# Attention values in the order of the head halves, and expert steps that turn the gathered rows two slots ahead

## The chip, the core and the metric

The kernel runs on one core of a Trainium2 chip. The metric is the time on the device, in microseconds (us), of one execution. Engines are named as the profile names them: PE (TensorE, with PEld for its weight loads), DVE (VectorE), ACT (ScalarE), POOL (GpSimd) and SP (SyncE, which only issues transfers here). Each engine works through its own list of instructions in order and waits on semaphores where it needs another's result.

## The reference

The input has 512 tokens of width 1024. Two blocks follow each other. Cut to what this change touches:

```python
# first block: sliding-window attention (4 heads, 2 key/value heads, blocks of 128 queries) and
# attention over 256 memory rows (4 heads)
out = einsum('bnhgqj,bnjhd->bnqhgd', probs, vb)          # sliding window
out = einsum('bhsm,bmhd->bshd', probs, mem_v)            # memory

# second block: attention over selected keys, 16 heads in 4 groups, 128 queries at a time
p = softmax(where(valid, logits, -inf))
o = einsum('bqhgk,bqkhd->bqhgd', p, v_sel)

# second block, last part: 32 experts (4 groups of 8), two of one group for each token, fp32
for g in range(4):
    a = einsum('nd,edf->nef', hf, w_gate[g])
    u = einsum('nd,edf->nef', hf, w_up[g])
    act = silu(a) * u * combine[:, g, :, None]
    out = out + einsum('nef,efd->nd', act, w_down[g])
return x + out
```

## The kernel before

It is one program for the whole of both blocks, with the list of each engine written out by hand. Nothing schedules it: the order of work on an engine is the order of the code. Two stages are touched.

**Attention.** `attention(...)` is PE's list for both attentions: 8 batches in the first (the four window blocks, then four blocks over the memory), 16 in the second (query block 3 first, then 2, 1 and 0, each for four groups of four heads). A batch b passes through these steps: scores (L764 or L839) into PSUM; DVE takes the maximum (L1656, L1663 or L1820); ACT takes the exponentials (L1173); PE turns the probabilities with a product by the identity (L740), heads 0 and 1 first and then, after the scores of a later batch, heads 2 and 3, through the same PSUM space `p_t`; the turned halves are copied to `pT`, the first by DVE (L1645, semaphore `pT_ready_first`), the second by ACT (L1233, `pT_ready_second`); a small product (L748) spreads the reciprocal of the denominators; the value products (`values1`, L771, or `values2`, L847) go to `p_v`; DVE multiplies them by the reciprocals (L1640, `y_made`). Before its value products PE waits for both halves of `pT` and for `y_made` of the batch before, which frees `p_v`. Keys reach 128 x (query block + 1), so in the second attention a batch has between 1 and 4 blocks of keys, and `values2` has two matmuls for each block, of 256 moving columns: heads 0 and 2 in one, heads 1 and 3 in the other. All of this is fp32; the trace has two records for each fp32 matmul.

**Experts.** The 32 experts are 16 pairs, and 8 further pairs take what exceeds 64 rows of an expert. They make 24 steps; slots 2, 5, 8, ... are the overflow pairs. In step s PE has `project(s)` (L1028: gate and up product of both experts of the pair, 16 matmuls of 512 columns from `xT`), `turn_slot(s + 1)` (L1020: eight transposes of the next slot's gathered rows `xg` into `p_rows`), `down(s - 1)` (L1040: eight matmuls of 512 columns from `actT`) and two transposes of the activations of step s (L1061). DVE copies `p_rows` to the single `xT` (L2148, after `turned` and after `gu_done` of the step, since `project` reads `xT`), and multiplies the activations (L2196). ACT applies silu (L1509), copies the down product to `yg` (L1503) and the turned activations to `actT` (L1513). POOL issues the indirect transfers: the gather of slot s + 3 (L1103, three buffers `xg`, after `turned`), at each third step, once the down product of the slot two back is done, the six transfers for the next overflow pair's weights (L1110, L1113), and the scatter of each slot's result (L1120). SP issues the plain loads of 1 MiB each for the weights: two of gate and up per expert after `gu_done` (L480), one of down per expert after `dn_done` (L483); `w_gu` and `w_dn` have three pairs of buffers. The step of index 0 has in addition a product that sorts the overflow rows (L1055).

Of the kernel before, what the change touches and what calls it, by code (L numbers as in the profile page):

```python
# [13 lines left out]
P = 128  # L14
# [8 lines left out]
HD = 64  # L23
# [14 lines left out]
STEPS = PAIRS + OVER_PAIRS  # L38
# [103 lines left out]
def program(nc, d, out):  # L142
# [11 lines left out]
    with ExitStack() as ctx:  # L154
# [30 lines left out]
        p_s, p_t, p_v, p_r = ps[1], ps[0][:, 0:2, :], ps[0][:, 2, :], ps[0][:, 3, :]  # L185


        base = -(-nc.sbuf_base // 64) * 64
# [40 lines left out]
        kvt = at("kvt", 48, [P, TT, 512])  # L229
# [284 lines left out]
        def _(pe):  # L514
# [119 lines left out]
            s = turns.take()  # L634
# [65 lines left out]
            def attention(batches, scores, values, nkb, pr, pT, base, first=None, beside=None):  # L700
# [8 lines left out]
                for i in range(batches + 2):  # L709
# [10 lines left out]
                            next(chunks)  # L720
                    b = i - 2
                    if 0 <= b < batches:
                        for half in range(2):
                            pe.wait_ge(pT_ready[half], base + b + 1)
                        if base + b > 0:
                            pe.wait_ge(y_made, base + b)
                        values(b, p_v).then_inc(v_full, 1)
                    b = i - 1
                    if 0 <= b < batches:
                        for half in range(2):  # L730
# [33 lines left out]
                    last = pe.matmul(s[:, h, 0:k.shape[1]], q, k, start=True, stop=True)  # L764
                return last

            def values1(b, out):
                blocks = 1 if b == 0 else 2
                for h, kb in ((2 * c + odd, kb) for c in range(2) for kb in range(blocks) for odd in range(2)):
                    v = sv1[:, max(b - 1, 0) + kb, HD * (h // 2):HD * (h // 2 + 1)] if b < 4 else mv[:, kb, HD * h:HD * (h + 1)]  # L770
                    last = pe.matmul(out[HD * (h % 2):HD * (h % 2 + 1), P * (h // 2):P * (h // 2 + 1)], v,  # L771
                                     pT1[:, h, P * kb:P * (kb + 1)], start=(kb == 0), stop=(kb == blocks - 1))
                return last
# [66 lines left out]
                                     kT2[g // 2][lanes, g % 2, 0:P * (n + 1)], start=True, stop=True)  # L840
                return last

            def values2(b, out):
                n, g = query_block(b), b % 4
                for kb in range(n + 1):
                    for odd in range(2):
                        last = pe.matmul(out[HD * odd:HD * (odd + 1), 0:256].rearrange("p (c t) -> p c t", c=2),  # L847
                                         kvt[:, kb, 256 + HD * g:256 + HD * (g + 1)], pT2[:, odd:4:2, P * kb:P * (kb + 1)],
                                         start=(kb == 0), stop=(kb == n))
                return last  # L850

# [109 lines left out]
            s = job()  # L961
# [53 lines left out]

            def turn_slot(s):

                pe.wait_ge(xg_in[s % 3], 16 * (s // 3 + 1))
                for k in range(KC):
                    last = pe.transpose(p_rows[:, k // 4, P * (k % 4):P * (k % 4 + 1)], xg[s % 3][:, k:D:KC], ident[:])  # L1020
                last.then_inc(turned, 1)
# [23 lines left out]
            for s in range(STEPS):  # L1045
                pe.wait_ge(xT_ready, s + 1)
                if s > 0:
                    pe.wait_ge(act_ready, s)
                project(s)
                if s + 1 < STEPS:  # L1050
                    turn_slot(s + 1)
                if s == 0:
                    pe.wait_ge(rt_step, 4)
                    for i in range(2 * TT):
                        last = pe.matmul(p_over, hot_r[:, i, :], over_c[:, i, :], start=(i == 0), stop=(i == 2 * TT - 1))  # L1055
                    last.then_inc(over_made, 1)
                if s > 0:
                    down(s - 1)
                pe.wait_ge(act_ready, s + 1)
                for f in range(2):  # L1060
                    last = pe.transpose(p_act[:, P * f:P * (f + 1)], act[:, f:HID:2], ident[:])  # L1061
                last.then_inc(act_turned, 1)
# [1160 lines left out]
```

## Time and profile before

| | |
|---|---|
| median of 3 runs | 1455.56 us (1453.52 to 1459.57) |
| the profiled execution | 1457.66 us, its span in the profile 1455.8 us |
| granted TensorE clock, mean of the span | 0.969 of full speed |
| PE busy | 1328.3 us, 91% of the span |
| POOL, DVE, ACT busy | 678.5, 579.4, 363.5 us |
| value products of the second attention (L847) | 160 records |
| gate and up products (L1028), busy | 172.0 us, 768 records |
| down products (L1040), busy | 87.6 us, 384 records |

A row of a timeline has the start, the duration, the engine, the line, the operation, output<-input, the tile's shape and how many instructions were merged; in brackets stands how long the engine had been idle and what released it. The durations of matmuls are modelled at their end, so that a matmul's record overlaps the next one's start by some 0.1 us: where a step's length matters it is read from one start to the next. In a line of waits the numbers are the total, the number of times and the longest. A release named "issue" is one for which the profile shows no other engine.

The first attention lies between about 183 and 227 us, the second between about 485 and 595 us, the experts between about 1128 and 1432 us.

### The profile page before, as it was taken

To read this page: it belongs to the slowest core of one execution; us is meant where nothing else is said; L and a number is where in the kernel's file an instruction comes from. 1 tells how busy PE (TensorE), PEld (TensorE's weight loads), DVE (VectorE), ACT (ScalarE), POOL (GpSimd) and SP (SyncE) were. 2 spreads that over 40 slices of the span, in tenths; PEclk is the share of its full clock that TensorE was granted. 3 is DMA by queue.
4 is the path that set the end of the run, shared out by engine and by line. 5 is a ranking of instruction groups with operands and counts; after the bars stand their busy time and mean duration, and the time that the engine had idled before them with its cause. 6 is when DMAs were issued, how large, how long until landed. Compare 5 with 4: busy or idle time off the path is not lost.

```text
span 1455.8 us, 18220 instructions
## 1 busy us (share of the span) xinstructions
PE 1328.3 (91%) x7169; PEld 954.5 (66%) x7169; DVE 579.4 (40%) x930; ACT 363.5 (25%) x707; POOL 678.5 (47%) x711
## 2 busy tenths in 40 slices
PE   5999979899899999999998888999995999999993
PEld 5887857777677666788887877888874333333330
DVE  1232262527891265534855566542314311111112
ACT  3201062402322277112123433231013011111110
POOL 6557513755547400676773233765851333333320
PEclk9999989999999999999999999999997999999997
DMA  5523210422123300134322113532273598999954
GB/s 207 147 73 116 66 51 7 139 98 88 60 85 116 112 6 1 58 95 145 108 72 73 44 44 131 222 140 87 87 317 131 192 384 354 366 372 369 373 220 188
DMA packets 85449, 216.34 MB, mean 149 GB/s; under 512 B 23716, under 2 KB 32628, under 8 KB 71796
## 3 DMA queue, kind: packets, MB, share of 16 engines
q1 hardware_dynamic: 62124, 199.22, 37.1%
q0 software_dynamic: 13824, 8.44, 2.0%
q10 hardware_dynamic: 9416, 7.51, 1.6%
q8 instruction: 57, 0.93, 0.3%
q14 instruction: 28, 0.23, 0.0%
HBM read 255.99 MB, written 26.22 MB: 194 GB/s over the span
## 4 chain that ended last, share of the span: by engine, by line
PE 78%; DVE 4%; ACT 4%; DMA 4%; issue 3%; POOL 2%; ACTq 2%; DVEq 1%; POOLq 0%; SPq 0%
PE ps L137 17%; PE ps L139 16%; PE ps L138 16%; PE ps L1028 9%; PE ps L1040 5%; DMA w_gu<-w_up,over_u 2%; PE ps L922 2%; PE ps L740 2%; PE ps L1020 2%; PE ps L847 1%; POOL w_lo L1073 1%; PE ps L839 1%; ACTq L1440 1%; DMA xg<-rows_scratch,row_u 1%; PE ps L748 1%
## 5 line engine op out<-in xcount | busy, mean ns | idle before, releaser
L1070 POOL CAST w_hi<-stage 128x512 fp32r<-128x512 f32 (+1 forms) x296 | 188.4, 678 | 490.3 <-PE ps L139 477.7
L1073 POOL TENSOR_TENSOR w_lo<-stage,w_hi 128x512 fp32r<-128x512 f32 (+1 forms) x296 | 386.5, 1337 | 10.8 <-issue 0.4
L137 PE MATMUL ps<-hi,w_hi 128*128 128x512 f32 (+1 forms) x600 | 234.8, 391 | 9.9 <-ACTq L1323 2.5
L139 PE MATMUL ps<-lo,w_hi 128*128 128x512 f32 (+1 forms) x600 | 233.3, 389 | 0.0
L138 PE MATMUL ps<-hi,w_lo 128*128 128x512 f32 (+1 forms) x600 | 233.1, 388 | 0.0
L137 PE MATMUL ps<-w_hi,hi 128*128 128x512 f32 (+2 forms) x520 | 187.9, 361 | 13.0 <-ACTq L1440 7.6
L138 PE MATMUL ps<-w_hi,lo 128*128 128x512 f32 (+2 forms) x520 | 186.3, 358 | 0.0
L139 PE MATMUL ps<-w_lo,hi 128*128 128x512 f32 (+2 forms) x520 | 186.2, 358 | 0.0
L1028 PE MATMUL ps<-w_gu,xT 128*64 128x512 f32 x768 | 172.0, 600 | 5.7 <-DMA w_gu<-w_up,over_u 4.3
L137 PEld LDWEIGHTS ps<-hi,w_hi 128*128 128x128 f32 x600 | 113.5, 189 | 37.6 <-issue 6.6
L139 PEld LDWEIGHTS ps<-lo,w_hi 128*128 128x128 f32 x600 | 113.3, 189 | 23.1
L138 PEld LDWEIGHTS ps<-hi,w_lo 128*128 128x128 f32 x600 | 113.6, 189 | 22.6
L2148 DVE TENSOR_TENSOR xT<-ps,ffn_kp 128x1024 f32<-128x1024 f32 x24 | 29.4, 1224 | 245.3 <-PE ps L1020 245.3
L1028 PEld LDWEIGHTS ps<-w_gu,xT 128*64 128x64 f32 x768 | 55.2, 138 | 104.8 <-issue 100.8
L137 PEld LDWEIGHTS ps<-w_hi,hi 128*128 128x128 f32 x520 | 100.7, 194 | 30.0 <-ACTq L1440 8.3
L139 PEld LDWEIGHTS ps<-w_lo,hi 128*128 128x128 f32 x520 | 100.6, 193 | 13.9
L138 PEld LDWEIGHTS ps<-w_hi,lo 128*128 128x128 f32 x520 | 100.6, 193 | 13.7 <-issue 0.2
L1040 PE MATMUL ps<-w_dn,actT 128*64 128x512 f32 x384 | 87.6, 598 | 1.0 <-ACT actT L1513 1.0
L1120 POOL DMA_INDIRECT y_scratch<-yg,out_u x24 | 24.2, 1007 | 114.2 <-ACT yg L1503 112.0
L1040 PEld LDWEIGHTS ps<-w_dn,actT 128*64 128x64 f32 x384 | 25.5, 136 | 45.5 <-issue 41.7
L1509 ACT ACTIVATE sa<-ps 128x256 f32<-128x256 f32 x24 | 9.2, 383 | 170.1 <-PE ps L1028 170.1
L1820 DVE CUSTOM_DVE_ANT_0 pr<-ps,sel 128x512 f32<-128x512 f32 (+3 forms) x64 | 27.6, 487 | 59.4 <-PE ps L839 53.8
(437 smaller groups left out, 1691.5 us busy)
## 6 DMA issues: line engine op xcount, KB each, us to landing
stage<-w_in SPq DMA_DIRECT2D x84, 512.0 KB, 4.5
w_gu<-w_gate SPq DMA_DIRECT2D x32, 1024.0 KB, 12.2
w_gu<-w_up SPq DMA_DIRECT2D x32, 1024.0 KB, 14.5
w_dn<-w_down SPq DMA_DIRECT2D x32, 1024.0 KB, 11.2
stage<-w_out SPq DMA_DIRECT2D x16, 512.0 KB, 4.5
stage<-w_ssd_branch SPq DMA_DIRECT2D x16, 512.0 KB, 4.5
stage<-w_in SPq DMA_DIRECT2D x20, 256.0 KB, 3.1
stage<-w_attn_branch SPq DMA_DIRECT2D x8, 512.0 KB, 4.3
```

What stands on the lines that cost most here:

```text
L137: pe.matmul(out, x[0], w[0], start=first, stop=False)
L138: pe.matmul(out, x[1], w[0], start=False, stop=False)
L139: return pe.matmul(out, x[0], w[1], start=False, stop=last)
L740: last = pe.transpose(p_t[:, h % 2, P * kb:P * (kb + 1)], pr(b)[:, h, P * kb:P * (kb + 1)], ident[:])
L922: last = pe.matmul(ps[s][:, h // 8, HD * (h % 8):HD * (h % 8 + 1)], decay[:, h, :], xd[:, h, :], start=True, stop=True)
L1020: last = pe.transpose(p_rows[:, k // 4, P * (k % 4):P * (k % 4 + 1)], xg[s % 3][:, k:D:KC], ident[:])
L1028: last = pe.matmul(p_gu[h], xT[:, k, h], w_gu[b][:, :, k, :], start=(k == 0), stop=(k == KC - 1))
L1040: last = pe.matmul(p_dn[h, c, :], actT[:, f, h], w_dn[b][:, f, 512 * c:512 * (c + 1)], start=(f == 0), stop=(f == 1))
L1070: nc.gpsimd.tensor_copy(hi[:, b, k, 0:n], stage[:, b, k, 0:n])
L1073: last = nc.gpsimd.tensor_tensor(lo[:, b, k, 0:n], stage[:, b, k, 0:n], hi[:, b, k, 0:n].bitcast(F32), ALU.subtract)
L1820: V.tensor_tensor_reduce(pr2[:, i % 2, h, 0:width], p_s[:, h, 0:width], sel[:, n, 0:width], 1.0, -3e38, ALU.add, ALU.max, sm[:, 0, k, h:h ...
L2148: V.tensor_tensor(xT[:], ps[0][:, 2:4, :].rearrange("p c (k t) -> p (c k) t", t=P), bc(ffn_kp[:], 2, P), ALU.mult)\
```

## The change

Two independent edits.

In `attention`, PE waits for `y_made` first, then for `pT_ready_first`, then runs the value products of heads 0 and 1 (half 0), then waits for `pT_ready_second`, then runs those of heads 2 and 3. `values2` therefore has matmuls of 128 moving columns, one per head and block of keys, twice as many as before; `values1` has the same matmuls as before, called half by half.

In the expert steps, step 0 and 1 still turn slot s + 1 behind `project(s)`. From step 1 on the rows of slot s + 2 are turned behind `down(s - 1)`, directly ahead of the transposes of the activations, and `turn_slot` waits until DVE has emptied `p_rows` (`xT_ready`). In steps 2 to 21 nothing stands between `project(s)` and `down(s - 1)`.

```diff
                     b = i - 2
                     if 0 <= b < batches:
+                        if base + b > 0:
+                            pe.wait_ge(y_made, base + b)
                         for half in range(2):
                             pe.wait_ge(pT_ready[half], base + b + 1)
-                        if base + b > 0:
-                            pe.wait_ge(y_made, base + b)
-                        values(b, p_v).then_inc(v_full, 1)
+                            last = values(b, half, p_v)
+                        last.then_inc(v_full, 1)
...
-            def values1(b, out):
+            def values1(b, c, out):
                 blocks = 1 if b == 0 else 2
-                for h, kb in ((2 * c + odd, kb) for c in range(2) for kb in range(blocks) for odd in range(2)):
+                for h, kb in ((2 * c + odd, kb) for kb in range(blocks) for odd in range(2)):
...
-            def values2(b, out):
+            def values2(b, c, out):
                 n, g = query_block(b), b % 4
                 for kb in range(n + 1):
                     for odd in range(2):
-                        last = pe.matmul(out[HD * odd:HD * (odd + 1), 0:256].rearrange("p (c t) -> p c t", c=2),
-                                         kvt[:, kb, 256 + HD * g:256 + HD * (g + 1)], pT2[:, odd:4:2, P * kb:P * (kb + 1)],
+                        last = pe.matmul(out[HD * odd:HD * (odd + 1), P * c:P * (c + 1)],
+                                         kvt[:, kb, 256 + HD * g:256 + HD * (g + 1)], pT2[:, 2 * c + odd, P * kb:P * (kb + 1)],
                                          start=(kb == 0), stop=(kb == n))
                 return last
...
             def turn_slot(s):
+                if s > 0:
+                    pe.wait_ge(xT_ready, s)
                 pe.wait_ge(xg_in[s % 3], 16 * (s // 3 + 1))
...
                 project(s)
-                if s + 1 < STEPS:
+                if s < 2:
                     turn_slot(s + 1)
...
                 if s > 0:
                     down(s - 1)
+                    if s + 2 < STEPS:
+                        turn_slot(s + 2)
                 pe.wait_ge(act_ready, s + 1)
```

PE's list in the second attention, one batch of query block 3 before (from the second half of a batch's transposes to the scores of another; `pr` are the probabilities, `sm` the reciprocals, `kvt` the values):

```order
L740 MATMUL ps<-ident,pr_107 128x128 [waits pT_ready_first]
L740 MATMUL ps<-ident,pr_107 128x128 x7
L748 MATMUL ps<-ident,sm 64x128 [waits share_ready,den_ready]
L748 MATMUL ps<-ident,sm 64x128 x3
L847 MATMUL ps<-pT_106,kvt 64x256 [waits y_made,pT_ready_second,pT_ready_first]
L847 MATMUL ps<-pT_106,kvt 64x256 x7
L740 MATMUL ps<-ident,pr_107 128x128 [waits pT_ready_second,exp_ready]
L740 MATMUL ps<-ident,pr_107 128x128 x7
```

And the same place with the change:

```order
L741 MATMUL ps<-ident,pr_107 128x128 [waits pT_ready_first]
L741 MATMUL ps<-ident,pr_107 128x128 x7
L749 MATMUL ps<-ident,sm 64x128 [waits share_ready,den_ready]
L749 MATMUL ps<-ident,sm 64x128 x3
L848 MATMUL ps<-pT_106,kvt 64x128 [waits pT_ready_first,y_made]
L848 MATMUL ps<-pT_106,kvt 64x128 x7
L848 MATMUL ps<-pT_106,kvt 64x128 [waits pT_ready_second]
L848 MATMUL ps<-pT_106,kvt 64x128 x7
L741 MATMUL ps<-ident,pr_107 128x128 [waits pT_ready_second,exp_ready]
L741 MATMUL ps<-ident,pr_107 128x128 x7
```

Eight matmuls of 256 columns became sixteen of 128, and the wait for the second half moved behind the first eight of them.

PE's list in the experts, the end of step 2 before (from the last matmul of its projection to the transposes of its activations):

```order
L1028 MATMUL ps<-w_gu_177,xT 64x512
L1020 MATMUL ps<-ident,xg_184 128x128 [waits xg_in0]
L1020 MATMUL ps<-ident,xg_184 128x128 x7
L1040 MATMUL ps<-w_dn_180,actT 64x512 [waits dn_in3,y_ready,dn_in2,actT_ready]
L1040 MATMUL ps<-w_dn_181,actT 64x512
L1040 MATMUL ps<-w_dn_180,actT 64x512
L1040 MATMUL ps<-w_dn_181,actT 64x512
L1040 MATMUL ps<-w_dn_180,actT 64x512
L1040 MATMUL ps<-w_dn_181,actT 64x512
L1040 MATMUL ps<-w_dn_180,actT 64x512
L1040 MATMUL ps<-w_dn_181,actT 64x512
L1061 MATMUL ps<-ident,act 128x128 [waits act_ready]
```

With the change:

```order
L1031 MATMUL ps<-w_gu_177,xT 64x512
L1043 MATMUL ps<-w_dn_180,actT 64x512 [waits dn_in3,y_ready,dn_in2,actT_ready]
L1043 MATMUL ps<-w_dn_181,actT 64x512
L1043 MATMUL ps<-w_dn_180,actT 64x512
L1043 MATMUL ps<-w_dn_181,actT 64x512
L1043 MATMUL ps<-w_dn_180,actT 64x512
L1043 MATMUL ps<-w_dn_181,actT 64x512
L1043 MATMUL ps<-w_dn_180,actT 64x512
L1043 MATMUL ps<-w_dn_181,actT 64x512
L1023 MATMUL ps<-ident,xg_185 128x128 [waits xg_in1,xT_ready]
L1023 MATMUL ps<-ident,xg_185 128x128 x7
L1066 MATMUL ps<-ident,act 128x128 [waits act_ready]
```

The eight transposes moved behind the down product, and they turn the next slot but one. The lists of the other engines are as before.

## Rows read from the trace of the kernel before

**Rows 1.** Page, part 4: the chain that ended last.

```profile
PE 78%; DVE 4%; ACT 4%; DMA 4%; issue 3%; POOL 2%; ACTq 2%; DVEq 1%; POOLq 0%; SPq 0%
```

**Rows 2.** Timeline, second attention, one batch of query block 3.

```profile
524.08 1.23 DVE L1645 COPY pT<-ps 128x1024 f32<-128x1024 f32 x1 [1.65 <-PE ps L740]
...
525.80 0.42 DVE L1640 TENSOR_TENSOR y<-ps,share 128x256 f32<-128x256 f32 x1 [0.17 <-issue]
...
526.49 0.66 PE L748 MATMUL ps<-ident,sm 128*64 128x128 f32 x8
526.60 1.02 ACT L1233 ACTIVATE pT<-ps 128x1024 f32<-128x1024 f32 x1 [1.34 <-PE ps L740]
...
527.72 1.95 PE L847 MATMUL ps<-pT,kvt 128*64 128x256 f32 x16 [0.57 <-issue]
```

**Rows 3.** Timeline of PE, first attention: matmuls of 128 columns.

```profile
208.35 1.09 PE L771 MATMUL ps<-pT,sv 128*64 128x128 f32 x16
```

**Rows 4.** Waits between 500 and 597 us, those of PE before L847.

```profile
PE ps L847 <- issue: 5.1, 10, 1.2
...
PE ps L847 <- ACT pT L1233: 0.7, 1, 0.7
```

**Rows 5.** Timeline of PE, first attention, values of batch 0.

```profile
193.61 1.12 PE L771 MATMUL ps<-pT,sv 128*64 128x128 f32 x8 [0.91 <-ACT pT L1233]
```

**Rows 6.** Chain in the first attention: start, duration, what.

```profile
213.77 1.50 ACTq L1247
```

**Rows 7.** Timeline of PE, expert step 3.

```profile
1168.90 7.09 PE L1028 MATMUL ps<-w_gu,xT 128*64 128x512 f32 x32
1175.92 1.16 PE L1020 MATMUL ps<-ident,xg 128*128 128x128 f32 x8
1177.01 3.65 PE L1040 MATMUL ps<-w_dn,actT 128*64 128x512 f32 x16
1180.59 0.51 PE L1061 MATMUL ps<-ident,act 128*128 128x128 f32 x2
1181.03 7.09 PE L1028 MATMUL ps<-w_gu,xT 128*64 128x512 f32 x32
```

**Rows 8.** Timeline of PE: step 0, whose transposes meet others, and step 23.

```profile
1139.89 1.16 PE L1020 MATMUL ps<-ident,xg 128*128 128x128 f32 x8
1140.80 1.03 PE L1055 MATMUL ps<-over_c,hot_r 128*128 128x8 f32 x8
...
1416.06 7.09 PE L1028 MATMUL ps<-w_gu,xT 128*64 128x512 f32 x32
1422.97 3.60 PE L1040 MATMUL ps<-w_dn,actT 128*64 128x512 f32 x16
1426.51 0.50 PE L1061 MATMUL ps<-ident,act 128*128 128x128 f32 x2
```

**Rows 9.** Timeline of POOL and PE around slot 3's gather in step 1.

```profile
1153.53 0.99 POOL L1103 DMA_INDIRECT xg<-rows_scratch,row_u  x1 [0.30 <-issue]
...
1156.34 0.50 PE L1061 MATMUL ps<-ident,act 128*128 128x128 f32 x2
```

**Rows 10.** DMA issues, window 1153.3 to 1154.3 us, that gather: count, us to landing.

```profile
xg<-rows_scratch,row_u POOLq DMA_INDIRECT x1, 4.2
```

**Rows 11.** Waits between 1130 and 1440 us: PE for an overflow pair's weights.

```profile
PE ps L1028 <- DMA w_gu<-w_up,over_u: 4.3, 4, 1.3
```

**Rows 12.** Timeline of POOL, and PE's: the second overflow pair's transfers and the projection that needs them.

```profile
1186.72 0.99 POOL L1110 DMA_INDIRECT w_gu<-w_up,over_u  x1 [0.30 <-issue]
...
1194.57 7.09 PE L1028 MATMUL ps<-w_gu,xT 128*64 128x512 f32 x32 [1.35 <-DMA w_gu<-w_up,over_u]
```

**Rows 13.** Windows, steps 1 to 21: us, busy of each engine, PEclk, DMA share, GB/s.

```profile
1143.20:1403.90 260.70, 254.97 (x1219) 97.32 (x1218) 32.98 (x45) 34.69 (x63) 84.05 (x84) 1.00 0.93 364
```

**Rows 14.** Gathers: POOL's issue after the overflow transfers, and the landing of all 24.

```profile
1190.63 1.02 POOL L1103 DMA_INDIRECT xg<-rows_scratch,row_u  x1 [0.30 <-issue]
...
DMA to landing us min/median/max: 3.4/10.0/11.4
```

## The prediction, made before the run

> **What bounds the kernel now.** I read the chain first: PE is 78% of it and no other engine has more than 4% [rows 1]. So time is won only where PE's own list gets shorter or where PE stands still. Next the timelines of the two stages, PE's rows first, then the row of whichever engine released a gap.
>
> In the second attention the reader should see PE finish its small product (start 526.49, modelled 0.66 us), stand still for 0.57 us, and begin the value products at 527.72, 0.10 us after ACT's copy of the second half (526.60 + 1.02 = 527.62). The first half was copied long before (DVE, 524.08 + 1.23 = 525.31), and `y_made` came at 526.22 [rows 2]. The waits name 5.1 us in 10 such gaps and 0.7 us in one more [rows 4].
>
> In the experts PE is nearly gapless. Step 3 is 7.02 (projection) + 1.09 (turn) + 3.58 (down) + 0.44 (activations) = 12.13 us from start to start [rows 7]. A matmul row's modelled end overlaps the next start by 0.07 (7.09 against 7.02). The only other losses are four waits for an overflow pair's weights, 4.3 us [rows 11], while the DMA engines are busy for 0.93 of the stage [rows 13].
>
> **Value products, second attention.** 160 records become 320, the columns stay. The price of a 128-column record comes from two rows of the same shape: 16 take 1.09, 8 take 0.66 [rows 2, 3], so one more costs (1.09 - 0.66)/8 = 0.054. Sixteen of 256 columns take 1.95 [rows 2]; thirty-two of 128 would take 1.09 + 16 x 0.054 = 1.95. The finer cut is free as long as the second half follows without a pause. I take 0; if each second half began afresh it would pay 1.09 - 16 x 0.054 - 0.07 = 0.16, for 16 batches 2.6 us.
>
> The gaps to be filled are 5.8 us, and each is 0.07 longer than its row says, because idle is counted from the modelled end: 11 x 0.07 = 0.8, so 6.6 us [rows 4]. Two can't be filled whole: the longest (1.2 + 0.07), since half a batch covers about 1.0 of it, leaves 0.3; the one behind ACT (0.7 + 0.07), where half a batch of one key block covers 0.3, leaves 0.5. That is 5.8. In the middle batches ACT's and DVE's own work nearly fills the shorter period; I take off 0.3 as an estimate: **5.5 us**, between 6.6 - 0.8 - 2.6 - 0.3 = 2.9 and 7.0. `y_made`, now waited for first, comes 0.85 before PE could start (526.22 against 526.49 + 0.66 - 0.07), so it holds nothing.
>
> *A rule against it.* The row says 0.054 us for a further 128-column product with its weight load. The Trainium skill ("TensorE: Matmul & The Clock Gate", section "Back-to-back issue gap") states sustained spacings of about 81 ns at 128 columns and 131 ns at 512. By an estimate from that page 320 products would take 25.9 us and 160 of 256 columns about 98 ns each, 15.7 us; the edit would pay 10.2 us to fill the gaps. The trace disagrees at 128 columns, and the sum goes by the trace.
>
> **Value products, first attention.** Counts don't change. Batch 0 waits 0.91 us for ACT before its 8 records [rows 5]; one half (about 0.5) moves into that gap: 0.5. In batches 4 to 7 the chain runs through ACT releasing the scores' PSUM (1.50 us as one piece [rows 6]), and an earlier value product is worth nothing there; only the last three batches have PE on the chain, about 0.2 each. **1.1 us**, between 0 and 1.4.
>
> **Expert steps.** No instruction is added or removed; three borders change.
> - Projection directly ahead of down: in step 23 the projection takes 1422.97 - 1416.06 = 6.91 instead of 7.02, and the down product behind it 1426.51 - 1422.97 = 3.54 instead of 3.58 [rows 7, 8]. 0.15.
> - Turn directly ahead of other full-width products: in step 0 the eight transposes take 1140.80 - 1139.89 = 0.91 instead of 1.09 [rows 7, 8]. 0.18.
>
> So 0.33 for each of steps 2 to 21, 6.6 us; step 1 has only the second (0.18), step 22 only the first (0.15): 6.9 us. The vacated place also frees `xT` and the activations earlier: DVE's copy starts as the projection ends and lies beside the 3.54 us of down.
>
> What the move costs: slot 3 is now turned at the end of step 1. Its gather is issued at 1153.53 and lands 4.2 us later, at 1157.73; PE arrives at 1156.34 [rows 9, 10]. PE waits 1.4 to 1.5 us, and the activations of step 1 and the whole of step 2 queue behind it. **Minus 1.5**; if it landed in the shortest time seen, 3.4 [rows 14], 0.6; if like the longest, 11.4, 8.6. Nothing else is in flight then, so I stay near 4.2. For later slots: the gather behind the overflow transfers is issued 1190.63 - 1180.59 = 10.0 us after its down product, and its rows are needed two steps later, 2 x 11.8 = 23.6; even 11.4 us to land leaves 2.2.
>
> The overflow weights: their transfers start when a down product ends, and the projection that needs them comes 0.44 + 12.13 = 12.57 later now, afterwards (0.91 + 0.44) + 6.91 + 3.54 + (0.91 + 0.44) = 13.15, so 0.58 more room. If they land by their own issue, the four waits shrink by 2.3. But the plain loads are released by the end of the projection ahead, and from there to the same point the way gets shorter, 17.24 to 16.69. The last needed transfer is issued at 1186.72 and PE starts at 1194.57, 7.8 later, though a gather alone lands in 4.2 [rows 10, 12]: it stands behind plain loads. Three steps contain 0.93 x 36.4 = 33.9 us of transfers [rows 13] and will last 3 x 11.8 = 35.4. If the backlog rules, six waits grow by 0.55 each: 3.3. I take **minus 1.0**, nearer the backlog.
>
> The Trainium skill ("DMA: Bandwidth & Descriptors", section "Queues, rings and completion order") says that each DMA engine takes turns between its queues packet by packet. By that POOL's transfers would not have to let the plain loads finish, the waits would shrink by those 2.3, and the total would be 3.3 better. The 7.8 against 4.2 speaks only half for it.
>
> Experts: 6.9 - 1.5 - 1.0 = **4.4 us**, between 6.9 - 1.5 - 3.3 = 2.1 and 6.9 - 0.6 + 2.3 = 8.6.
>
> **Sum.** 5.5 + 1.1 + 4.4 = 11.0 us. The profiled execution took 1457.66 (span 1455.8), 2.1 over the median shown; I subtract from the median: 1455.56 - 11.0 = **1444.5 us**. The bounds together give 1438.5 to 1450.6; the stages between are PE's and should pass a gain on.
>
> **Rivals.**
> 1. *The experts turn into a DMA stage.* For: share 0.93, and each load is released by PE, so that the queues run empty for a while in every three steps whatever PE does. Against: 33.9 us fit into 35.4. Then the shorter steps come back as longer waits on `w_gu`, and the stage gives nothing: 1448.9.
> 2. *The second attention is not PE's.* ACT or DVE would take the place of the gap. For: their rows fill most of a batch. Against: ACT stood idle 1.34 and DVE 1.65 in the batch shown [rows 2]. Half a gain, 2.0 instead of 5.5: 1448.0.
> 3. *The finer products are slow.* If a 128-column product cost what the rows of the transposes give, 0.91/8 = 0.114 each [rows 8], 320 would take 36.5 instead of 320 x 0.054 = 17.3: 19.2 paid and 5.8 filled, so 13.4 lost instead of 5.5 won: 1463.4, slower. It decides above (17.3 + 5.8 + 5.5)/320 = 0.089 us each. Against: the records of [rows 3] have the very shape. By the Trainium skill's spacings, above, 10.2 would be paid and 5.8 filled, 4.4 lost, and the time 1454.4; with the trace against it that has 0.02.
> 4. *Gathers late behind the loads*, in each third step; it needs more than 13.5 us to land, and 11.4 is the longest. With 16 us six stalls of 2.5 us: 1459.5.
> 5. *More than I count*: the waits on overflow weights vanish and the borders in the attention also shorten: 1439.
>
> **Chances.** Forecast with its own bounds (1440 to 1449) 0.60; the first rival 0.15, the second 0.08, the third 0.03 (and 0.02 for its case by the Trainium skill), the fourth 0.03, the fifth 0.09. To hold the time 8 times in 10 the range reaches from 1438.5 to 1451.5. Within 0.5% is within 7.3 us, about what a measurement of this kernel tells from no change: faster than 1448.3 has 0.57 + 0.05 + 0.05 + 0.09 = 0.76, slower than 1462.8 the third and a part of the fourth, 0.04, the rest 0.20.
>
> **What would show it.** In the second attention PE's rows should run from the small product straight into the first half, with no "issue" ahead of it, batches of block 3 some 0.6 us shorter, and 320 records with some 0.055 between starts. In the experts a step of 11.8 us, transposes and activations 1.35 together, one wait on the gather in step 1 of 1.5 us, and waits on `w_gu` of 3 to 8 us in all. I am wrong if the steps stay at 12.1, if the waits on `w_gu` or `xg` exceed 10 us, or if ACT's idle in the attention goes to nothing while the batches keep their length.

## The result, and the profile after

| | before | changed |
|---|---|---|
| median | 1455.07 us (1453.52 to 1459.57, 4 runs) | 1439.71 us (1438.15 to 1444.75, 4 runs) |
| profiled execution (span) | 1457.66 us (1455.8 us) | 1438.15 us (1436.3 us) |
| granted TensorE clock, mean | 0.969 | 0.971 |

The ratio is 0.9893 [0.9865, 0.9922]: the change takes 15.6 us off, between 11.3 and 19.6 by the interval. The forecast was 1444.5 us (11.0 off), its range 1438.5 to 1451.5.

The chain of the changed kernel, page, part 4, which answers to [rows 1]:

```profile
PE 77%; ACT 5%; DMA 5%; DVE 5%; issue 3%; POOL 2%; ACTq 2%; DVEq 1%; POOLq 0%; SPq 0%
```

PE still bounds the kernel, so again only PE's rows have to be followed. To compare two executions I cut PE's list into stretches by landmarks that both have (first score product of each attention, product behind the last values, first projections, last down product) and took the differences of start times:

| stretch, us | before | changed | difference |
|---|---|---|---|
| start to the first attention | 182.75 | 181.90 | -0.85 |
| first attention | 44.38 | 43.06 | -1.32 |
| from there to the second | 257.72 | 255.25 | -2.47 |
| second attention | 110.14 | 103.82 | -6.32 |
| to the projection of step 0 | 535.99 | 535.80 | -0.19 |
| projection 0 to projection 1 | 12.22 | 12.28 | +0.06 |
| projection 1 to the last down | 284.77 | 276.75 | -8.02 |

The three touched stages give 1.3 + 6.3 + 8.0 = 15.6 us. The profiled spans differ by 19.5; the other 3.9 lie in stretches that no line of the change touches. That the three stages give the very 15.6 of the medians is chance: further profiles, below, make it 14.0.

*Second attention.* PE's timeline of the changed kernel, the batch that answers to [rows 2] (block 3, the last of its four batches, as there; start, us, engine, line, what):

```profile
519.55 0.66 PE L749 MATMUL ps<-ident,sm 128*64 128x128 f32 x8
...
520.04 1.92 PE L848 MATMUL ps<-pT,kvt 128*64 128x128 f32 x32
...
521.88 0.88 PE L741 MATMUL ps<-ident,pr 128*128 128x128 f32 x6
```

From the small product to the row behind the values it takes 521.88 - 519.55 = 2.33 us. In the kernel before it took 3.11, from 526.49 to the row behind those of [rows 2]:

```profile
529.60 0.66 PE L740 MATMUL ps<-ident,pr 128*128 128x128 f32 x4
```

There is no gap ahead of L848. From the values of the batch in front to these it is 6.02 us (514.02 to 520.04) where it was 6.65 (521.07 to 527.72), so 0.63 of the 0.78 us stay and 0.15 are given back elsewhere in the batch; the prediction had asked for some 0.6. ACT's copy of the second half, which runs 519.66 to 520.68, lies beside the first half of the values:

```profile
519.66 1.02 ACT L1238 ACTIVATE pT<-ps 128x1024 f32<-128x1024 f32 x1 [0.71 <-PE ps L741]
```

PE's group of the values in this attention, by line (busy, mean ns of one, idle time before them and its releasers), in the kernel before:

```profile
L847 PE MATMUL ps<-pT,kvt 128*64 128x256 f32 x160 | 20.8, 387 | 6.1 <-issue 5.1 <-ACT pT L1233 0.7
```

The same in the changed kernel, and there PE's waits before the values (us, times, longest), which answer to [rows 4]:

```profile
L848 PE MATMUL ps<-pT,kvt 128*64 128x128 f32 x320 | 21.9, 276 | 1.0 <-ACT pT L1238 0.8
```

```profile
PE ps L848 <- ACT pT L1238: 0.8, 3, 0.3
```

The idle time before the values fell from 6.1 us to 1.0, and none of it is "issue" any more.

*First attention.* The values of batch 0, which answer to [rows 5], and the chain at a middle batch, which answers to [rows 6]:

```profile
191.64 0.64 PE L772 MATMUL ps<-pT,sv 128*64 128x128 f32 x4
192.68 0.70 PE L772 MATMUL ps<-pT,sv 128*64 128x128 f32 x4 [0.39 <-ACT pT L1238]
193.30 1.12 PE L741 MATMUL ps<-ident,pr 128*128 128x128 f32 x4
```

```profile
207.97 1.50 ACTq L1252
```

Half of batch 0's values went into the gap, and 0.39 of the 0.91 us is left. The middle batches have still the 1.50 us of ACT on the chain, and their period is 4.71 us in both kernels (205.90 to 210.61 before, 204.81 to 209.52 now, PE's score products).

*Experts.* PE's timeline of one step, which answers to [rows 7]:

```profile
1237.48 3.60 PE L1043 MATMUL ps<-w_dn,actT 128*64 128x512 f32 x16
1241.01 1.16 PE L1023 MATMUL ps<-ident,xg 128*128 128x128 f32 x8
1242.00 0.40 PE L1066 MATMUL ps<-ident,act 128*128 128x128 f32 x2
1242.34 7.09 PE L1031 MATMUL ps<-w_gu,xT 128*64 128x512 f32 x32
1249.25 3.60 PE L1043 MATMUL ps<-w_dn,actT 128*64 128x512 f32 x16
```

From start to start: projection 6.91, down 3.53, slot's transposes 0.99, activations' transposes 0.34, together 11.77 (before 7.02 + 3.58 + 1.09 + 0.44 = 12.13). The waits of PE from 1130 us on, which answer to [rows 11]:

```profile
PE ps L1031 <- DMA w_gu<-w_up,over_u: 2.5, 5, 0.6
PE ps L1023 <- DMA xg<-rows_scratch,row_u: 2.3, 1, 2.3
```

Two of the prediction's signs missed here. It asked for 3 to 8 us of waits on `w_gu`, and the row has 2.5; and it placed one wait of 1.5 us on slot 3's rows, while the row is that of slot 2. What the DMA engines did in the steps between projection 1 and projection 22, which answers to [rows 13]:

```profile
1132.10:1386.10 254.00, 249.10 (x1229) 100.73 (x1228) 32.98 (x45) 37.58 (x63) 84.53 (x85) 1.00 0.95 374
```

The share rose from 0.93 to 0.95, as the same transfers in shorter steps must make it.

And step 1, in which slots 2 and 3 are both turned (it answers to [rows 9]):

```profile
1141.46 1.12 PE L1023 MATMUL ps<-ident,xg 128*128 128x128 f32 x8 [2.27 <-DMA xg<-rows_scratch,row_u]
1142.51 3.65 PE L1043 MATMUL ps<-w_dn,actT 128*64 128x512 f32 x16
1146.25 1.13 PE L1023 MATMUL ps<-ident,xg 128*128 128x128 f32 x8
```

The start of slot 3's transposes is 3.74 us behind that of the down product, which takes 3.58 elsewhere: 0.16 us of wait on slot 3 are left.

### The profile page after: what moved, and what is told of

Same layout as the page of the kernel before. It is cut to its first block, busy times and chain, and to the rows that moved or that the text cites. A ratio compares the mean times of both kernels' runs of the same rounds, so it can differ in the third digit from the quotient of the medians.

```text
span 1436.3 us, 18562 instructions
## 1 busy us (share of the span) xinstructions
PE 1318.1 (92%) x7329; PEld 961.5 (67%) x7329; DVE 575.2 (40%) x930; ACT 365.1 (25%) x707; POOL 677.5 (47%) x711
## 4 chain that ended last, share of the span: by engine, by line
PE 77%; ACT 5%; DMA 5%; DVE 5%; issue 3%; POOL 2%; ACTq 2%; DVEq 1%; POOLq 0%; SPq 0%
PE ps L137 17%; PE ps L139 16%; PE ps L138 16%; PE ps L1031 9%; PE ps L1043 5%; DMA w_gu<-w_up,over_u 3%; PE ps L923 2%; PE ps L741 2%; POOL w_lo L1078 1%; PE ps L1023 1%; PE ps L848 1%; PE ps L840 1%; ACT pr L1178 1%; DMA xg<-rows_scratch,row_u 1%; ACTq L1445 1%
## 5 line engine op out<-in xcount | busy, mean ns | idle before, releaser
L1043 PEld LDWEIGHTS ps<-w_dn,actT 128*64 128x64 f32 x384 | 28.8, 137 | 53.6 <-issue 52.3
## 6 DMA issues: line engine op xcount, KB each, us to landing
w_gu<-w_up SPq DMA_DIRECT2D x32, 1024.0 KB, 14.5
```

The costliest lines, as they stand in the source:

```text
L1043: last = pe.matmul(p_dn[h, c, :], actT[:, f, h], w_dn[b][:, f, 512 * c:512 * (c + 1)], start=(f == 0), stop=(f == 1))
```

## The experiments

Seven kernels. All ratios are to the kernel before. The profile of each gives the same stretches as above; where runs of one kernel spread over several us, it is the stretch that tells more than the median.

**The attention's edits alone** (e_attention): the changed kernel with the expert steps of before.

```
-                if s > 0:
-                    pe.wait_ge(xT_ready, s)
...
-                if s < 2:
+                if s + 1 < STEPS:
...
-                    if s + 2 < STEPS:
-                        turn_slot(s + 2)
```

> The kernel before with the attention edit alone. Lengths by starts: second attention (first score product to the product behind the last values) 110.1 us before and 103.8 with both edits; first attention 44.3 and 43.0; the stretch between them 257.8 and 255.3; step 1 to the last down product of the experts 284.8 and 276.7. Theory: the two edits don't touch each other, and the stretch between the attentions varies from run to run by itself. Then the second attention is 103.8 +- 0.3, the first 43.0, the experts stay at 284.8 +- 1, and the time is 7.5 us below before (5 to 10). Rival: a part of the gain is handed on, since after a shorter first attention the stretch behind it also gets shorter (the weights are split further ahead); then that stretch is 255.3 again here, and 257.8 in the kernel with the expert edit alone.

Measured: 1444.6 us (1442.66 to 1449.32, 6 runs), ratio 0.9932 [0.9914, 0.9951], so 9.9 us. The attention stages are 43.26 and 103.84 us long, those of the changed kernel within 0.2; the stretch from projection 1 to the last down is 283.68. The two attentions give 1.1 + 6.3 = 7.4 us by their lengths, which the interval of the ratio (7.1 to 12.5 us) holds as well as the 9.9. The stretch between the attentions is 255.6 here, and 257.9 in the next kernel, which is what the rival had said of a gain handed on; e_fine and e_best speak against it further down. Its PE waits from 1130 us on, with the expert steps of before:

```profile
PE ps L1029 <- DMA w_gu<-w_up,over_u: 2.4, 3, 1.1
PE ps L1021 <- DMA xg<-rows_scratch,row_u: 2.1, 1, 2.1
```

**The expert steps alone** (e_experts): the value products as before.

```
-                            last = values(b, half, p_v)
-                        last.then_inc(v_full, 1)
+                        values(b, p_v).then_inc(v_full, 1)
```

> The kernel before with the expert edit alone. Theory: all that the experts gained is theirs: steps of 11.78 us instead of 12.13, six waits for an overflow pair's weights of 3.0 us in all (2.5 to 3.5) instead of 4.6, 276.7 us from step 1 to the last down product, and a time 8 us below before (6 to 10); the attentions stay at 44.3 and 110.1. Rival: the smaller waits on overflow weights were chance of one execution, since the plain loads in the way are the same; then the waits come out between 4 and 8 us and the stage at 278 to 282.

Measured: 1449.42 us (1447.19 to 1450.7), ratio 0.9963 [0.9948, 0.9977], so 5.4 us, less than expected. Stretches: attention 44.67 and 110.16 (44.38 and 110.14 before), experts 278.02, 6.75 shorter than before. Neither expected answer fits whole: the waits of 3.3 us are still those of the theory, the stage is at the lower edge of the rival's 278 to 282. The two parts add up, 9.9 + 5.4 = 15.3 against 15.6, but each is known to 2 or 3 us only. Its PE waits from 1130 us on:

```profile
PE ps L1030 <- DMA w_gu<-w_up,over_u: 3.3, 3, 1.4
PE ps L1022 <- DMA xg<-rows_scratch,row_u: 2.9, 2, 2.1
```

**The finer products without the overlap** (e_fine): expert steps of before, value products by halves, but both halves awaited ahead of the first.

```
+                        for half in range(2):
+                            pe.wait_ge(pT_ready[half], base + b + 1)
                         for half in range(2):
-                            pe.wait_ge(pT_ready[half], base + b + 1)
                             last = values(b, half, p_v)
```

> Only the finer cut of the value products, with both waits still ahead of the first of them: 320 records of 128 columns in the second attention. Theory: a further product of 128 columns costs 0.054 us, so a batch of four key blocks spends 32 x 0.054 + 0.15 = 1.88 us from its first value product to the next work, as with 16 of 256 columns; second attention 110.1 +- 1 us, time as before. Rival (a weight load paired with each product sets the pace, 0.081 us): 2.6 us for such a batch, 320 x 0.081 = 25.9 against 18, second attention 118 us, time 8 us above before.

Measured: 1455.12 us (1448.77 to 1456.16, 10 runs), ratio 1.0006 [0.9989, 1.0023]; second attention 110.34 us against 110.14, first 44.57 against 44.38. The profiled execution is the fastest of the ten. A batch of block 3 and PE's group in this kernel:

```profile
520.84 0.66 PE L750 MATMUL ps<-ident,sm 128*64 128x128 f32 x8
522.07 1.97 PE L849 MATMUL ps<-pT,kvt 128*64 128x128 f32 x32 [0.57 <-issue]
523.97 0.87 PE L742 MATMUL ps<-ident,pr 128*128 128x128 f32 x6
```

```profile
L849 PE MATMUL ps<-pT,kvt 128*64 128x128 f32 x320 | 21.0, 276 | 6.1 <-issue 5.1 <-ACT pT L1235 0.7
```

The 320 records carry the very idle time that 160 carried before (6.1: 5.1 and 0.7 named, as in [rows 4]), and 32 records take 523.97 - 522.07 = 1.90 us where 16 of 256 columns took 529.60 - 527.72 = 1.88. So the cut into halves is free within 0.2 us a stage, and the attention's gain comes from the overlap it allows. The third rival (slow finer products) is out. The stretch between the attentions is 255.0 us here, without any gain in the first attention. The old expert steps take 282.65 us from projection 1 to the last down, and their PE waits from 1130 us on are a third sample:

```profile
PE ps L1030 <- DMA w_gu<-w_up,over_u: 2.1, 3, 1.2
PE ps L1022 <- DMA xg<-rows_scratch,row_u: 1.5, 1, 1.5
```

**Turning only one slot ahead, behind down** (e_one_ahead): value products as before.

```
-                if s < 2:
+                if s == 0:
...
-                    if s + 2 < STEPS:
-                        turn_slot(s + 2)
+                    if s + 1 < STEPS:
+                        turn_slot(s + 1)
```

> The kernel before with the rows of the next slot, not of the next but one, turned behind the down product from step 1 on; the three borders between kinds of products are then as in the changed kernel, but DVE can fill xT only at the step's end. Theory: the borders win 0.35 us a step, and PE waits in each step for DVE (1.22 for xT, 0.41 for the activations, and 0.2 of hand-overs, less nothing that hides it): 12.13 - 0.35 + 1.8 = 13.6 us a step, experts 284.8 + 22 x 1.45 = 317 us, less 4 for waits on weights that vanish, time 28 us above before. Rival: most of the copy hides behind the transposes of the activations, and a step is 12.3 or less, time within 4 us of before; turning two ahead would then be worth little beyond the borders.

Measured: 1493.94 us (1493.28 to 1494.48), ratio 1.0267 [1.0248, 1.0287], so 39 us slower where 28 were expected; a step takes 13.76 us instead of the expected 13.6, steps 1 and 2 take 16.94 and 16.44. Its waits of PE between 1160 and 1480 us, one step, and DVE's rows in it:

```profile
PE ps L1065 <- DVE act L2200: 36.4, 21, 2.1
```

```profile
1196.02 3.60 PE L1042 MATMUL ps<-w_dn,actT 128*64 128x512 f32 x16
1199.55 1.16 PE L1022 MATMUL ps<-ident,xg 128*128 128x128 f32 x8
1202.42 0.51 PE L1065 MATMUL ps<-ident,act 128*128 128x128 f32 x2 [1.72 <-DVE act L2200]
1202.86 7.09 PE L1030 MATMUL ps<-w_gu,xT 128*64 128x512 f32 x32
```

```profile
1200.82 1.23 DVE L2152 TENSOR_TENSOR xT<-ps,ffn_kp 128x1024 f32<-128x1024 f32 x1 [12.21 <-PE ps L1022]
1201.96 0.41 DVE L2200 TENSOR_TENSOR act<-sa,ps 128x256 f32<-128x256 f32 x1
```

The same order of PE's products with the turn for the next slot instead of the next but one: now DVE's copy of `xT` can begin only when the turn ends, DVE's product for the activations stands behind that copy on its list, and PE waits 1.72 us for it ahead of the activations' transposes in most steps. The wait also takes away the borders between the two kinds of transposes: the eight take 2.87 - 1.72 = 1.15 us (1199.55 to 1202.42), the two 0.44, as when they stood apart. The new place is worth its 0.35 us only because the slot is turned a step earlier.

**Overflow weights issued early** (e_gu_early), and **in another order** (e_gu_first). In both, the overflow pair's transfers are split in `overflow_gu` (four) and `overflow_dn` (two). e_gu_first calls one behind the other in the old place; e_gu_early moves the first ahead of the wait for down:

```
                         pool.wait_ge(gu_done, s)
+                        overflow_gu(s // 3)
                         pool.wait_ge(dn_done, s)
-                        overflow(s // 3)
+                        overflow_dn(s // 3)
```

> The changed kernel, with one thing moved on POOL's list: in each third step the overflow pair's four w_gu transfers are issued as soon as the projection that last read their buffers has ended, and only its two w_dn transfers wait for the down product. The w_gu issues come 3.5 us earlier (the down product's length in the changed kernel). Theory (the remaining waits of PE on overflow weights, 2.5 us in five places of 0.34 to 0.65, are a matter of when POOL issues them): all of them vanish, the stretch from the projection of step 1 to the last down product falls from 276.8 to some 274, and the kernel takes 2.5 to 3 us less than the changed one, a ratio to the kernel before of 0.987. Rival (the plain loads of SP's queue ahead of them set the landing, since the DMA engines are busy 0.93 of the stage or more): the waits stay at 2 to 3 us or move to the w_gu of plain slots, and the ratio is that of the changed kernel, 0.989.

> The changed kernel, with the overflow pair's six transfers in another order and none issued earlier: four w_gu, then two w_dn. The last w_gu goes out as the fourth instead of the fifth, 1.3 us earlier. Theory (landing follows POOL's own issue): a wait of 0.34 to 0.65 us that is 1.3 us late in its issue vanishes, so 2.5 us of waits go to nothing, as with the early issue. Rival (the backlog of plain loads sets the landing): the waits stay between 0.3 and 0.7 us each. Either way the stage moves by 0 to 2.5 us, so the rows of the waits tell, not the time.

Measured: e_gu_early 1437.29 us (1435.9 to 1440.02, 6 runs), ratio 0.9892 [0.9873, 0.9912]; e_gu_first 1437.97 us (1437.31 to 1438.44, 4 runs), 0.9894 [0.987, 0.9918]. By the time neither can be told from the changed kernel. By PE's waits from 1130 us on they can; first e_gu_first, then e_gu_early, which has no row for `w_gu` (nor has e_best, the next kernel):

```profile
PE ps L1031 <- DMA w_gu<-w_up,over_u: 3.0, 4, 1.1
PE ps L1023 <- DMA xg<-rows_scratch,row_u: 2.8, 2, 1.5
```

```profile
PE ps L1023 <- DMA xg<-rows_scratch,row_u: 2.7, 2, 1.5
```

The early issue takes all of the waits away. It is 8.0 us earlier and not the 3.5 that I expected (POOL's first issue of the same pair at 1233.95 us, against 1241.95): the projection that frees the buffers is that of the step before, so POOL doesn't stand at that wait at all, and the four `w_gu` transfers go out ahead of the plain loads, which follow at 1237.83; the two of `w_dn` stay behind, at 1242.03. This edit moves the time and the place ahead of the plain loads together, and no run parts the two. The stretch to the last down falls to 274.16 us (276.75 in the changed kernel, 277.49 in e_gu_first), 2.6 us for the 2.5 of waits. The order alone takes nothing away, though the last `w_gu` leaves 1.3 us earlier. One pair of the changed kernel shows why: POOL's rows, then the landing of the issues at 1245.83 and 1247.13 us and of the last at 1248.42, and PE's row.

```profile
1241.95 0.99 POOL L1115 DMA_INDIRECT w_gu<-w_gate,over_u  x1 [8.47 <-PE ps L1043]
...
1247.13 0.99 POOL L1115 DMA_INDIRECT w_gu<-w_up,over_u  x1 [0.30 <-issue]
1248.42 0.99 POOL L1118 DMA_INDIRECT w_dn<-w_down,over_u  x1 [0.30 <-issue]
```

```profile
w_gu<-w_gate,over_u POOLq DMA_INDIRECT x1, 7.0
...
w_gu<-w_up,over_u POOLq DMA_INDIRECT x1, 7.6
...
w_dn<-w_down,over_u POOLq DMA_INDIRECT x1, 6.4
```

```profile
1254.83 7.09 PE L1031 MATMUL ps<-w_gu,xT 128*64 128x512 f32 x32 [0.64 <-DMA w_gu<-w_up,over_u]
```

They land at 1252.8, 1254.7 and 1254.8, the last two together; the last plain load, issued at 1239.01, lands 15.1 later, at 1254.1. The order of issue is gone on arrival: the last of POOL's transfers and the last plain load end within 0.7 us of each other. Measured from the first of the pair's six issues, PE's late starts are at 12.0 to 13.0 us in the three profiles with the old steps (before, e_attention, e_fine) and at 12.6 to 13.7 in the three with the new ones (changed, e_experts, e_gu_first). Measured from the first plain load of the same step, they are at 17.5 to 18.5 and 16.8 to 17.9. Neither distance stays the same, which the two expected answers had not foreseen: the landing follows neither POOL's issue nor the plain loads alone. That all of it ends together when the queues run dry is my reading and not shown by a run of its own.

**With slot 3's gather ahead** (e_best): e_gu_early, and

```
+            pool.wait_ge(turned, 1)
+            gather(3)
...
             pool.wait_ge(over_ready, 1)
             gather(2)
...
-                if s + 3 < STEPS:
+                if 0 < s < STEPS - 3:
```

> The early issue of the overflow pair's w_gu, and besides the gather of slot 3 moved forward: it goes out right behind the turning of slot 0, ahead of the overflow work of the first slots, instead of in step 0's place on POOL's list. It is measured whether slot 3's rows still hold the transposes at the end of step 1, and whether slot 2's gather, now behind it, gets later. Theory: the step from projection 0 to projection 2 (27.7 us in the changed kernel, with 2.3 us of waits on slot 2's rows and 0.2 on slot 3's) loses at most 0.2 on slot 3 and pays up to 1.3 us (one issue) on slot 2: no gain over the early issue alone. Rival: the rows of slot 2 wait for the counts of overflow and not for POOL's queue, so slot 2 doesn't move, and the stretch gets 0.2 to 0.8 us shorter.

Measured: 1437.54 us (1434.25 to 1438.38, 5 runs), ratio 0.9883 [0.9861, 0.9905], no gain that can be told. The wait on slot 3 is gone, and slot 2's gather isn't later (issued 5.8 us before PE comes for it, as in the other kernels). But the stretch from projection 1 to projection 2 is 16.76 us, longer than the 15.82 of e_gu_early. PE's timeline and the granted clock by windows (us, busy of PE, PEld, DVE, ACT, POOL, PEclk, DMA share, GB/s) say why:

```profile
1142.17 1.94 PE L1023 MATMUL ps<-ident,xg 128*128 128x128 f32 x8 [2.12 <-DMA xg<-rows_scratch,row_u]
1144.05 4.41 PE L1043 MATMUL ps<-w_dn,actT 128*64 128x512 f32 x16
1148.39 1.16 PE L1023 MATMUL ps<-ident,xg 128*128 128x128 f32 x8
```

```profile
1132.00:1142.00 10.00, 7.52 (x34) 2.52 (x34) 1.20 (x8) 0.77 (x2) 5.95 (x6) 1.00 0.98 396
1142.00:1148.30 6.30, 6.13 (x24) 2.81 (x24) 1.55 (x2) 0.00 (x0) 1.98 (x2) 0.73 0.15 33
```

Behind the wait of 2.12 us the granted clock is 0.73 of full speed, so a part of this stretch ran at the lower of its two levels (1.2 and 2.4 GHz), and the transposes and the down product take 1.88 + 4.34 = 6.22 us where they took 1.05 + 3.58 = 4.63 in step 1 of the changed kernel (above, without the 0.16 us of wait). Against e_gu_early the wait on slot 3 (1.24 us) is gone, slot 2's is 2.12 instead of 1.48, and 1.6 us are lost at the lower clock: together 1.0 us more, which is the difference. The changed kernel kept 1.00, the upper level, behind a wait of 2.27 us:

```profile
1141.00:1147.00 6.00, 5.45 (x31) 2.80 (x32) 1.55 (x2) 0.79 (x1) 2.97 (x3) 1.00 0.30 75
```

So one execution of each doesn't say that this happens in every run. The first attention takes 42.1 us here, the shortest of all nine kernels, and the stretch behind it is 257.4 all the same.

## Why the prediction was right, and where its sizes were off

**The mechanism held in all three stages**, and the chain stayed PE's. The measured gain is 4.6 us above the 11.0 forecast. The time of 1439.71 lies 1.2 us inside the fast end of the stated range, and just outside the 1440 to 1449 that had the chance of 0.60. Five terms were taken too low for the gain, by 0.8, 0.2, 0.5, 0.5 and 1.0 us, together 3.0; the remaining 1.6 us have no term, and that the time still fell inside the range owes something to luck.

*"each is 0.07 longer than its row says"*, second attention. Forecast 5.5, measured 6.3. The 0.07 was the overlap of a large product's modelled end. In front of these gaps stands the small product of eight, and its row of 0.66 us is followed by the next start after 520.04 - 519.55 = 0.49: the overlap is 0.17. So the gaps held 5.8 + 11 x 0.17 = 7.7 us instead of 6.6, and 0.8 left over as forecast (1.0 by the row) would make 6.9; 0.6 less came out, where I had taken off 0.3 for ACT's and DVE's own work. The 0.15 us that a batch of block 3 gives back, above, is of this kind; what holds each batch I haven't traced. (The upper bound of 7.0 stood above the 6.6 us that I had in the gaps, with no term for it.) The zero for the finer cut was right by e_fine (0.2 us of 110). The Trainium skill ("TensorE: Matmul & The Clock Gate", section "Back-to-back issue gap") has about 81 ns at 128 columns; here 32 such records take 1.90 us, 0.059 each, and 320 of them change nothing, while 256 columns take 1.88/16 = 0.118 where the estimate between the page's two figures had 0.098; the measurement decides against the page for this form (weights of 64 columns).

*First attention*: forecast 1.1, measured 1.3 in the pair of the table (44.4 to 44.7 us in the four kernels with the value products of before or of e_fine, 42.1 to 43.3 in the five others). Batch 0 gained 0.5 as said (191.58 to 194.67 before, 190.73 to 193.30 now); the last two periods 0.36 us each (217.77 to 221.62 before, 216.36 to 219.85 now), where I had taken three of 0.2.

*Borders of the experts*: 0.35 for each of the twenty steps (12.13 to 11.78) instead of 0.33; steps 1 and 22 gave 0.4 together. 7.4 us instead of 6.9. The 0.18 that I had put on the slot's transposes came as 0.10 there and 0.10 on the two of the activations.

*"PE waits 1.4 to 1.5 us"* for slot 3. The step failed: slot 3 waited 0.16 us, and slot 2, for which I had nothing, waited longer than before. Slots 2 and 3 must be taken together: their gathers leave 9.07 us apart, and PE now does only a turn and a down product between them, so a long wait on the first shortens the second. In three profiles with the old steps slot 2 costs 1.4, 2.1 and 1.5 us; in four with the new ones (e_best, with another order, left out) the two cost 2.4, 2.9, 2.8 and 2.7. The difference of the means is 1.0. The row of [rows 10], 4.2 us to land, was used; slot 3's gather landed in 3.7.

*"I take minus 1.0, nearer the backlog"*, the overflow weights. This step failed. The pair of profiles shown has 4.3 us before and 2.5 after, which looks like a gain; but two other profiles with the old steps (e_attention and e_fine) have 2.4 and 2.1, and e_experts and e_gu_first with the new ones 3.3 and 3.0. The means are 2.9 and 2.9. By the lengths of the steps, which count the shortest waits too, it is 4.6, 2.8 and 2.4 us with the old steps and 2.9, 3.7 and 3.2 with the new ones, 3.3 and 3.3 in the mean. The waits moved neither way by an amount that six profiles can tell. The working had the two answers right (issue follows down: 0.58 more room; plain loads follow the projection: 0.55 less) but asked which of them rules. By e_gu_first it is neither of the two alone; that both releases enter, through the moment when the queues run dry, stays a reading. The case by the Trainium skill ("DMA: Bandwidth & Descriptors", section "Queues, rings and completion order": queues are served in turns, packet by packet) fits the fact that POOL's group and the plain loads end together; the 2.3 us that I derived from it did not come.

Together the experts' own gain is 7.4 - 1.0 - 0 = 6.4 us, between e_experts' 5.4 [3.3, 7.6] and the 8.0 of the pair of profiles; the waits of the overflow weights, 1.7 us apart in that pair by the step lengths, make that difference. The lengths from projection 1 to the last down say the same without any terms: 284.77, 283.68 and 282.65 us with the old steps, 276.75, 278.02 and 277.49 with the new ones, in the mean 6.3 us less. With 7.6 in the attentions this is 14.0 us, inside the interval of the ratio. **What stays open** is the rest up to 15.6. The profiles differ besides in the stretch between the attentions: 257.4 to 257.9 us in four kernels (before, e_experts, e_one_ahead, e_best), 255.0 to 255.6 in four (changed, e_attention, e_fine, e_gu_early), and 253.1 in e_gu_first. No edit goes with these groups, since e_best and e_gu_first have the same code up to there as the changed kernel; it is a spread between executions. One place holds all of the 2.5 us by which the pair of the table differs, transposes that neither edit touches, first before, then changed:

```profile
274.33 8.14 PE L617 MATMUL ps<-unit_a,xres 128*128 128x128 f32 x56 [2.50 <-DVEq L1706]
```

```profile
270.91 6.67 PE L617 MATMUL ps<-unit_a,xres 128*128 128x128 f32 x56 [1.25 <-DVEq L1711]
```

The wait for DVE is 1.25 us shorter, and the granted clock over the 6.6 us behind it is 1.00 instead of 0.74, which is worth 1.5. From the first of these transposes to the product behind them it takes 14.2 to 14.5 us in the four kernels with 257 us, 11.7 to 11.8 in changed, e_attention and e_fine, and 12.9 in e_gu_early and e_gu_first, where the wait is 2.4 and the clock 1.00. Why DVE comes later in some executions is not shown.

**The rivals.** The first (the experts turn into a DMA stage, 1448.9) is out: the steps came down to 11.77 and the waits on `w_gu` didn't grow, though the DMA share rose to 0.95, near the 33.9/35.4 = 0.96 that the prediction's own figures give. There is little room left beyond it. The second (attention not PE's) is out: no "issue" gap is left, and the batches became 0.63 us shorter. The fourth (gathers late in each third step) is out: no PE wait on `xg` behind step 1. The fifth, more than counted, at 1439, is nearest to the measured time, but not for its reason: the waits on the overflow weights did not vanish.

## What to carry to other kernels

Where PE waits for the second of two copies, cutting its product along the copies fills the gap, and the cut costs nothing here (0.2 us in 110); what it gains is read from start to start, since the overlap of a row's modelled end depends on the kind of product in front of the gap. Moving transposes next to others of the same width pays 0.2 us a time, but only if nothing has to wait for their result in between: here it was needed a full step later. Two waits at the head of a pipeline share their length, and waits on a busy queue must be read from several profiles before a difference of 1 or 2 us in them is put down to an edit; what shortened them here was to issue the four awaited transfers 8 us earlier, ahead of the plain loads, and not another order within the group.

## What the runs showed of the hardware

- Sustained products of 128 columns with a weight load of 64 columns each: 0.059 us a record (32 in 1.90 us), the same time for the same columns as at 256 (16 in 1.88 us).
- Borders between kinds of products: transposes behind a projection and ahead of a down product take 1.09 us for eight, behind a down product and ahead of two other transposes 0.99; the two 0.34 instead of 0.44; a projection followed by a product of its own kind 6.91 instead of 7.02.
- The last two of six transfers of POOL's queue, issued 1.3 us apart behind 4 MB of plain loads, landed within 0.1 us of each other; with `w_gu` moved forward within the group PE waited as long (3.0 us against 2.5), with the four `w_gu` issued 8 us earlier and ahead of the plain loads it never waited.
- After an idle of PE of 2.12 us in step 1 the granted clock was 0.73 over 6.3 us in one kernel, and 1.00 after 2.27 us in another. Between the attentions it was 0.74 over 6.6 us after a wait of 2.50 us, and 1.00 after one of 2.45 us in e_gu_early.
